# Seven products in place of eight: one Strassen level in the up projection of blocks 1 to 3

## The chip, the cores and the metric

The kernel runs on one core of one Trainium2 chip. The metric is the device time of the whole program in microseconds. Shorter is better. The engines are called here as the profile calls them: PE is the matmul engine (PEld its weight loads), ACT the scalar engine, DVE the vector engine, POOL the GpSimd engine, SP the engine that issues nearly all transfers. Each of them works through its own queue in order.

## The reference, cut to what matters

One decoder layer over 2048 tokens of width 1024, all float32: a gated linear attention mixer beside a cross-attention, an output projection, and then the MLP that the change touches.

```python
def sq_relu_mlp(h, w_up, w_down):
    u = jax.nn.relu(h @ w_up)
    return (u * u) @ w_down
...
    x = x + sq_relu_mlp(rms_norm(x, norm_mlp[i]), w_up[i], w_down[i])
return rms_norm(x, final_norm)
```

Here h is 2048 x 1024, w_up 1024 x 4096 and w_down 4096 x 1024.

## The kernel before

The tokens are taken in four blocks of 512 (block 0 to 3), and each block passes through the mixer, the output projection and the MLP before the next one starts. Every float32 operand is kept as two parts, a high one (`h_hi`, `w_hi`, `u_hi`) that the matmul takes as it is and a low one that holds the remainder (`h_lo`, `w_lo`, `u_lo`). A product of two operands is then three matmuls, high by high, high by low and low by high (`product`, L2171 to L2176); each has a 128 x 128 stationary tile of its own. For weights the parts are made in flight: SP loads a chunk of 1 MB into one of two slots of `raw` (`load`, L739 to L743), ACT copies it into `w_hi` (`split_hi`, L1019, or by halves `split_hi_piece`, L1025), DVE subtracts (`split_lo`, L1517, `split_lo_piece`, L1523). The load of chunk i waits until chunk i - 2 has been split. The two halves of a chunk are its pieces.

The MLP of a block has 16 up chunks of 256 hidden features and 4 groups of 7 down chunks (list `MLP`, L143 to L147). An up chunk multiplies 1024 x 256 weights with 512 tokens, as 2 feature tiles x 8 k-blocks x 3 matmuls of 512 columns, into banks 0 and 1. The down projection already goes by one Strassen (Winograd) level: for each group of 4 up chunks there are 7 products `M1` to `M7` (`PRODUCTS`, L122), each of 24 matmuls of 512 columns. Their operands are three quarters of u (`A11`, `A12`, `A22`) and four sums of quarters (`S1` to `S4`); the sums of the down weights are made once in block 0 by DVE (`mix_sums`, L1504) and kept in DRAM (`w_mix`), and SP issues the loads and stores for them in block 0 (`mix_work`, L767).

Between an up chunk and the down products stands the chain that makes the seven operands of u for one chunk, in the single buffer `u_parts` (8 tiles of 128 x 256): ACT takes relu and square of each bank (`relu_square`, L1384), DVE makes the four sums (`u_sums`, L2028), ACT copies the 3 and the 4 tiles into `u_hi` (`u_high`, L1395), DVE subtracts (`u_low`, L2038, which raises `u_ready`). The next chunk's relu waits for `u_ready` of the chunk before, since it writes `u_parts` again. The operands go into a ring of 5 chunks (`RING`), and the first up chunk of the next group runs ahead of a group's down chunks.

The first up chunk of a block is special (`first_up_chunk`, L2590): it takes its 512 tokens as two halves of 256, since h is only just being transposed, and so has 96 matmuls of 256 columns.

In the MLP, POOL has only small work: reciprocal roots of the norms (`rsqrt`, L912), a diagonal for the next block, and in the last group of blocks 0 to 2 the scaling of the next block's columns (L1010), 8 instructions of 128 x 512.

In the last group of a block PE takes its two first down products by pieces (`last_group_start`, L2664): k-blocks 0, 1 and 2 of both, and then k-block 3 of each, so that the last up chunk has more time to get ready.

## Time and profile before

| | us |
|---|---|
| median of 3 runs | 2530.14 (2529.99 to 2530.43) |
| span of the profiled execution | 2527.2 |
| what lies around the span (2530.14 less 2527.2) | 2.9 |
| PE busy | 2490.0 (99%) |
| DVE busy | 1691.7 (67%) |
| ACT busy | 1247.7 (49%) |
| POOL busy | 345.9 (14%) |
| mean granted clock of PE | 0.999 of full |

The span runs from the first to the last instruction. A busy time is the time in which an engine had an instruction under way. The profiled execution's own device time is not given apart from the span, so the median stands for it: the two differ by 2.9 us, 0.1%. A row of a timeline has the start, the duration, the engine, the line, the operation with what it writes and reads, the shape and how many instructions in a row it merges; in brackets stands idle time before it and what ended that.

### The profile page before, as it was taken

The page shows a single profiled execution, that of the slowest core. Times are in us where ns is not written, and L with a number is a line of the kernel's source. Part 1 is how long each engine was busy: PE and PEld are TensorE (multiplying, and loading weights), DVE is VectorE, ACT ScalarE, POOL GpSimd, SP SyncE. Part 2 cuts the span into 40 slices and gives each one's busy share as a digit, 9 for nine tenths or more (in the row PEclk, how much of TensorE's full clock was granted, in tenths as well). Part 3 has the DMA queues.
Part 4 walks back from the last instruction along what each step waited for, and adds up shares of the span by engine and source line. Part 5 has one row for each costly group of instructions (what it writes and reads, how often), then busy time and mean ns, then how long its engine had stood idle before and what let it go on. Part 6 is the DMA issues. An engine that isn't in the chain of part 4 may idle for free.

```text
span 2527.2 us, 31134 instructions
## 1 busy us (share of the span) xinstructions
PE 2490.0 (99%) x11724; PEld 2087.1 (83%) x11724; DVE 1691.7 (67%) x2473; ACT 1247.7 (49%) x1832; POOL 345.9 (14%) x328
## 2 busy tenths in 40 slices
PE   8999999999999999999999999999999999999998
PEld 7888887888788888888888888888888888888887
DVE  5677467566767786665566778656665687765566
ACT  5544354544554455455455445545455445554344
POOL 0034200000304320000110431000020143000000
PEclk9999999999999999999999999999999999999999
DMA  8522458555732143544442215354444213443443
GB/s 292 183 84 67 157 194 304 182 205 171 261 134 67 51 175 117 190 144 133 166 168 82 67 56 203 100 183 150 150 167 147 70 59 107 160 134 120 164 150 133
DMA packets 201681, 369.48 MB, mean 146 GB/s; under 512 B 8032, under 2 KB 120032, under 8 KB 192576
## 3 DMA queue, kind: packets, MB, share of 16 engines
q1 hardware_dynamic: 200912, 367.25, 43.0%
q8 instruction: 95, 1.56, 0.2%
q14 instruction: 50, 0.41, 0.1%
q10 hardware_dynamic: 624, 0.27, 0.0%
HBM read 336.03 MB, written 31.46 MB: 145 GB/s over the span
## 4 chain that ended last, share of the span: by engine, by line
PE 86%; DVE 5%; DMA 3%; ACT 2%; issue 2%; POOL 1%; DVEq 0%; SPq 0%; ACTq 0%; POOLq 0%
PE banks L2174 25%; PE banks L2175 25%; PE banks L2176 25%; PE banks L2348 3%; POOL queries L946 1%; PE banks L2387 1%; PE banks L2391 1%; PE banks L2327 1%; DVE w_lo L1527 1%; PE banks L2372 1%; PE banks L2304 1%; DMA xres<-in_x 1%; DMA raw<-w_out_mix 1%; DVE xres L1928 0%; DVE query_dec L1679 0%
## 5 line engine op out<-in xcount | busy, mean ns | idle before, releaser
L2174 PE MATMUL banks<-h_hi,w_hi 128*128 128x512 f32 (+1 forms) x1728 | 666.5, 386 | 3.3 <-issue 1.3
L2176 PE MATMUL banks<-h_hi,w_lo 128*128 128x512 f32 (+1 forms) x1728 | 659.0, 381 | 0.0
L2175 PE MATMUL banks<-h_lo,w_hi 128*128 128x512 f32 (+1 forms) x1728 | 659.0, 381 | 0.0
L1527 DVE TENSOR_TENSOR w_lo<-raw,w_hi 128x1024 fp32r<-128x1024 f32 x284 | 357.6, 1294 | 105.2 <-ACT w_hi L1030 97.6
L1520 DVE TENSOR_TENSOR w_lo<-raw,w_hi 128x2048 fp32r<-128x2048 f32 x122 | 292.6, 2398 | 149.2 <-ACT w_hi L1023 145.4
L1030 ACT ACTIVATE w_hi<-raw 128x1024 fp32r<-128x1024 f32 x248 | 253.9, 1053 | 279.3 <-PE banks L2174 93.0
L2174 PEld LDWEIGHTS banks<-h_hi,w_hi 128*128 128x128 f32 x1728 | 324.9, 188 | 66.2 <-issue 4.8
L2176 PEld LDWEIGHTS banks<-h_hi,w_lo 128*128 128x128 f32 x1728 | 324.8, 188 | 63.3
L2175 PEld LDWEIGHTS banks<-h_lo,w_hi 128*128 128x128 f32 x1728 | 325.0, 188 | 60.9
L2174 PE MATMUL banks<-w_hi,u_hi 128*128 128x512 f32 x896 | 350.9, 392 | 2.3 <-DVE w_lo L1527 1.8
L2176 PE MATMUL banks<-w_hi,u_lo 128*128 128x512 f32 x896 | 349.4, 390 | 0.0
L2175 PE MATMUL banks<-w_lo,u_hi 128*128 128x512 f32 x896 | 349.2, 390 | 0.0
L1023 ACT ACTIVATE w_hi<-raw 128x2048 fp32r<-128x2048 f32 x122 | 233.6, 1915 | 145.0 <-PE banks L2174 121.0
L1928 DVE TENSOR_TENSOR xres<-banks,xres 128x512 f32<-128x512 f32 x274 | 182.0, 686 | 75.3 <-PE banks L2176 74.4
L1390 ACT ACTIVATE u_parts<-banks 128x512 f32<-128x512 f32 x128 | 76.2, 595 | 294.7 <-PE banks L2176 163.6
L2174 PEld LDWEIGHTS banks<-w_hi,u_hi 128*128 128x128 f32 x896 | 168.6, 188 | 39.4 <-issue 3.7
L2175 PEld LDWEIGHTS banks<-w_lo,u_hi 128*128 128x128 f32 x896 | 168.6, 188 | 35.4 <-issue 0.7
L2176 PEld LDWEIGHTS banks<-w_hi,u_lo 128*128 128x128 f32 x896 | 168.4, 188 | 35.4
L2033 DVE TENSOR_TENSOR u_parts<-u_parts 128x256 f32<-128x256 f32 x64 | 27.2, 426 | 240.6 <-ACT u_parts L1393 240.6
L946 POOL TENSOR_TENSOR queries<-q,query_dec 128x384 f32<-128x384 f32 x144 | 144.9, 1034 | 175.3 <-ACT query_dec L1172 108.1
L915 POOL TENSOR_TENSOR rstd<-ms,minus_half 128x1 f32<-128x1 f32 x44 | 28.3, 646 | 1027.4 <-DVE ms L1542 1023.2
L2174 PE MATMUL banks<-w_hi,h_hi 128*128 128x512 f32 x392 | 158.8, 405 | 1.6 <-ACT v L1142 1.6
(237 smaller groups left out, 3485.7 us busy)
## 6 DMA issues: line engine op xcount, KB each, us to landing
raw<-in_w_up SPq DMA_DIRECT2D x64, 1024.0 KB, 5.7
raw<-w_mix SPq DMA_DIRECT2D x64, 1024.0 KB, 4.7
raw<-in_gla_w_in SPq DMA_DIRECT2D x56, 1024.0 KB, 5.1
raw<-in_w_down SPq DMA_DIRECT2D x48, 1024.0 KB, 5.1
raw<-w_out_mix SPq DMA_DIRECT2D x24, 512.0 KB, 4.3
raw<-in_w_out SPq DMA_DIRECT2D x21, 512.0 KB, 3.7
xin<-in_w_down SPq DMA_DIRECT2D x10, 1024.0 KB, 5.1
w_mix<-xin SPq DMA_DIRECT2D x10, 1024.0 KB, 5.3
```

Source lines behind the costliest of these rows:

```text
L915: nc.gpsimd.tensor_tensor(rstd[:, which, t:t + 1], ms[:, which, t:t + 1], minus_half[:, 0:1], ALU.pow).then_inc(rstd_ready.sem, 1)
L946: last = nc.gpsimd.tensor_tensor(kind_cols(queries, w, kind), spans(at_chunk(q, c), w, first, count), kind_cols(query_dec, w, kind), ALU.mult)
L1023: nc.scalar.activation(w_hi[:, i % 2, :], raw[:, i % 2, :], ACT.Copy).then_inc(hi_split.sem, PIECES)
L1030: nc.scalar.activation(w_hi[:, i % 2, at], raw[:, i % 2, at], ACT.Copy).then_inc(hi_split.sem, 1)
L1390: nc.scalar.activation(part, banks[:, f, :].rearrange("p (h t) -> p h t", h=2), ACT.Relu)\
L1520: nc.vector.tensor_tensor(w_lo[:, i % 2, :], raw[:, i % 2, :], w_hi[:, i % 2, :].bitcast(F32), ALU.subtract).then_inc(lo_split.sem, PIECES)
L1527: nc.vector.tensor_tensor(w_lo[:, i % 2, at], raw[:, i % 2, at], w_hi[:, i % 2, at].bitcast(F32), ALU.subtract).then_inc(lo_split.sem, 1)
L1928: nc.vector.tensor_tensor(xres[:, t, cols], bank(name), xres[:, t, cols], ALU.add)\
L2174: after_chunk(pe.matmul(to, left[0], right[0], start=start, stop=False, skip_group_check=goes_on))
L2175: pe.matmul(to, left[0], right[1], start=False, stop=False, skip_group_check=goes_on)
L2176: return pe.matmul(to, left[1], right[0], start=False, stop=stop, skip_group_check=goes_on)
L2348: ins = pe.matmul(bank(name)[:, (h % 2) * COLS:(h % 2 + 1) * COLS], left, queries[:, h, :], start=True, stop=True)
```

## The change

Blocks 1 to 3 get another order of steps (`LATE_MLP`). Up chunks 0 and 1 stay as they are. Each up chunk from 2 to 15 becomes two steps, "up a" and "up b", that together make 7 products of 4 k-blocks x 3 matmuls of 256 columns: the tokens are halved (256 and 256), the width of h is halved (4 and 4 k-blocks) and the chunk's 256 features are halved. `M1`, `M6`, `M7` and `M4` are added up in one bank (0 or 7 by turns), `M5` and `M3` share bank 1, and `M2` has bank 6. The output quarters are put together on the way: ACT keeps copies of the bank after `M1`, `M6` and `M5` (`keep_part`), and DVE adds `M2`, `M7` and `M3` to them (`add_part`). The four sums of h are made once a block, two by DVE and two by POOL (both called `h_sums`), and split by ACT and DVE (`s_high`, `s_low`). The squares of three of the u quarters and the four sums of u go from ACT and DVE to POOL (`late_squares`); the fourth quarter is squared by ACT (`corner`). The sums of the up weights are made by POOL in block 0 (`up_mix`, 4 instructions of 128 x 512 a chunk, 14 chunks) and stored to DRAM (`w_up_mix`), and the late steps load them: 1.75 MB a chunk, 0.75 MB of it in runs of 128 columns (512 bytes), where a chunk was 1 MB in runs of 1 KB. The ring of u operands has 4 chunks instead of 5, no up chunk runs ahead of a group's down chunks, and every group of blocks 1 to 3 now starts with the order that only the last group had (`group_start`). The next block's rows of x are loaded one at a time for their squares (`load_x_row`) instead of all at once. Block 0 keeps its steps, with `up_mix` and the stores added; `gain_fin` is loaded later there.

```diff
+
+PLAIN_UPS = 2
+LATE_UPS = UPS - PLAIN_UPS
+LATE_RING = DEPTH
+
+LATE_UP_A = (("M1", A11, 0), ("M2", A12, 1), ("M6", S2, 2), ("M5", S1, 3))
+LATE_UP_B = (("M7", S3, 1), ("M3", S4, 0), ("M4", A22, 2))
+LATE_MLP = []
+for _g in range(GROUPS):
+    for _c in range(DEPTH * _g, DEPTH * (_g + 1)):
+        LATE_MLP += [("up", _c)] if _c < PLAIN_UPS else [("up a", _c), ("up b", _c)]
+    LATE_MLP += [("down", _g, j) for j in range(len(PRODUCTS))]
...
+def late_bank(c, name):
+
+    return {"M2": 6, "M5": 1, "M3": 1}.get(name, 7 if c % 2 else 0)
...
+            def up_mix_store(c):
+
+                sp.wait_ge(up_mix_made, c - PLAIN_UPS + 1)
+                sp.dma_start(w_up_mix[:, c - PLAIN_UPS, 0:2, :], up_mix_t2_t1).then_inc(up_mix_stored, 16)
+                sp.dma_start(w_up_mix[:, c - PLAIN_UPS, 2:4, :], up_mix_t3_t4).then_inc(up_mix_stored, 16)
+
+            def load_late(n, s):
+
+                i, what = OTHERS.mlp + s, LATE_MLP[s]
+                if what[0] not in ("up a", "up b"):
+                    load(n, i, *late_weights(s))
+                    return
+                sp.wait_ge(*hi_split.at(n, last_piece(i - 2)))
+                sp.wait_ge(*lo_split.at(n, last_piece(i - 2)))
+                c, to = what[1], raw[:, i % 2, :]
+                cols = wup[:, :, FCOLS * c:FCOLS * (c + 1)]
+                if what[0] == "up a":
+                    sp.dma_start(to[:, 0:1024].rearrange("p (k c) -> p k c", k=KD), cols[:, :, 0:P])                        .then_inc(up_part_loaded[i % 2].sem, 16)
+                    sp.dma_start(to[:, 1024:2048].rearrange("p (e x) -> p e x", e=2), w_up_mix[:, c - PLAIN_UPS, 0:2, :])                        .then_inc(raw_loaded[i % 2].sem, 16)
+                else:
+                    sp.dma_start(to[:, 0:512].rearrange("p (k c) -> p k c", k=KG), cols[:, KG:KD, P:2 * P])                        .then_inc(up_part_loaded[i % 2].sem, 16)
+                    sp.dma_start(to[:, 512:1536].rearrange("p (e x) -> p e x", e=2), w_up_mix[:, c - PLAIN_UPS, 2:4, :])                        .then_inc(raw_loaded[i % 2].sem, 16)
...
                                 sp.wait_ge(mix_stored[slot], 16 * made)
+                    if s >= 2 and MLP[s - 2][0] == "up" and MLP[s - 2][1] >= PLAIN_UPS:
+                        up_mix_store(MLP[s - 2][1])
...
+                        load_next_columns(n, x_col)
+                        sp.wait_ge(up_mix_stored, 32 * LATE_UPS)
+                        sp.dma_start(gain_fin[:], final_norm.rearrange("(a d) -> a d", a=1).broadcast_to([P, D]))\
+                            .then_inc(gain_fin_loaded, 16)
...
+                def up_mix(s, c):
+
+                    i = FIRST.mlp + s
+                    w = as_kblocks(raw, i % 2, KD)
+                    b11, b12, b21, b22 = (w[:, KG * r:KG * (r + 1), P * f:P * (f + 1)] for r in range(2) for f in range(2))
+                    t2, t1, t3, t4 = (e[:, j, :].rearrange("p (k c) -> p k c", k=KG)
+                                      for e in (up_mix_t2_t1, up_mix_t3_t4) for j in range(2))
+                    pool.wait_ge(*raw_loaded[i % 2].at(n, i // 2))
+                    if c > PLAIN_UPS:
+                        pool.wait_ge(up_mix_stored, 32 * (c - PLAIN_UPS))
+                    pool_link(nc.gpsimd.tensor_tensor(t1, b12, b11, ALU.subtract))
+                    pool_link(nc.gpsimd.tensor_tensor(t2, b22, t1, ALU.subtract))
+                    nc.gpsimd.tensor_tensor(t3, b22, b12, ALU.subtract)
+                    nc.gpsimd.tensor_tensor(t4, b21, t2, ALU.subtract).then_inc(up_mix_made, 1)
+
+                def h_sums():
+
+                    pool.wait_ge(*read(n, ("hT", 1, KD // 2 - 1)))
+                    pool.wait_ge(*read(n, ("hT", 0, KD // 2 - 1)))
+                    a11_hi, a11_lo = (e[:, 0:KG, early_h].bitcast(F32) for e in (h_hi, h_lo))
+                    a21_hi, a21_lo = (e[:, 0:KG, late_h].bitcast(F32) for e in (h_hi, h_lo))
+                    a12_hi, a12_lo = (e[:, KG:KD, early_h].bitcast(F32) for e in (h_hi, h_lo))
+                    nc.gpsimd.tensor_tensor(s3_sum[:], a11_hi, a21_hi, ALU.subtract)
+                    pool_link(nc.gpsimd.tensor_tensor(s3_part[:], a11_lo, a21_lo, ALU.subtract))
+                    nc.gpsimd.tensor_tensor(s3_sum[:], s3_sum[:], s3_part[:], ALU.add).then_inc(s34_sum_ready.sem, 1)
+                    pool.wait_ge(*s12_sum_ready.at(n, 1))
+                    pool_link(nc.gpsimd.tensor_tensor(s4_sum, a12_hi, s2_sum[:], ALU.subtract))
+                    nc.gpsimd.tensor_tensor(s4_sum, s4_sum, a12_lo, ALU.add).then_inc(s34_sum_ready.sem, 1)
+
+                def late_squares(c):
+
+                    a1, b1, b2, a2, s1, s2, s3, s4 = (u_parts[:, e, :] for e in range(8))
+                    k = c - PLAIN_UPS
+                    pool.wait_ge(*relu_ready.at(n, k))
+                    nc.gpsimd.tensor_tensor(u_parts[:, 0:3, :], u_parts[:, 0:3, :], u_parts[:, 0:3, :], ALU.mult)\
+                        .then_inc(body_ready.sem, 1)
+                    pool.wait_ge(*body_ready.at(n, k))
+                    pool.wait_ge(*corner_ready.at(n, k))
+                    pool_link(nc.gpsimd.tensor_tensor(s1, a2, b2, ALU.add))
+                    nc.gpsimd.tensor_tensor(s3, a1, a2, ALU.subtract)
+                    pool_link(nc.gpsimd.tensor_tensor(s2, s1, a1, ALU.subtract))
+                    nc.gpsimd.tensor_tensor(s4, b1, s2, ALU.subtract).then_inc(sums_ready.sem, 1)
+
+                for t in range(TILES):
+                    rsqrt(n, 0, t)
+                if first:
+                    for s, what in enumerate(MLP):
+                        if what == ("up", 2 * DEPTH + 1):
+                            for t in range(TILES):
+                                rsqrt(n, 1, t)
+                            diagonals()
+                        if what[0] == "up" and what[1] >= PLAIN_UPS:
+                            up_mix(s, what[1])
+                else:
+                    h_sums()
+                    for c in range(PLAIN_UPS, UPS):
+                        late_squares(c)
+                        if n < BLOCKS - 1 and c % DEPTH == DEPTH - 1 and c // DEPTH in (1, 2):
+                            for t in range(2 * (c // DEPTH) - 2, 2 * (c // DEPTH)):
+                                rsqrt(n, 1, t)
+                    if n < BLOCKS - 1:
+                        diagonals()
+                if n < BLOCKS - 1:
...
+                def late_up(s, c):
+
+                    ahead = c - 1 if c % DEPTH else None
+                    after = s + 2
+                    if c == PLAIN_UPS:
+                        relu_square(1, 1)
+                    elif ahead is not None:
+                        corner(ahead)
+                    late_split_hi(s + 1, 0)
+                    if c == PLAIN_UPS:
+                        s_high(S4)
+                    keep_part(c, "M1")
+                    late_split_hi(s + 1, 1)
+                    keep_part(c, "M6")
+                    if ahead is not None:
+                        u_high(ahead, False)
+                    late_split_hi(after, 0)
+                    keep_part(c, "M5")
+                    late_split_hi(after, 1)
+                    if ahead is not None:
+                        u_high(ahead, True)
+                    late_relu(c)
+
+                def late_down(s, g, j):
+
+                    c, more = DEPTH * g + DEPTH - 1, s + 1 < len(LATE_MLP)
+                    if j == 0:
+                        corner(c)
+                        late_split_hi(s + 1, 0)
+                        late_split_hi(s + 1, 1)
+                        u_high(c, False)
+                        late_split_hi(s + 2, 0)
+                        u_high(c, True)
+                    elif j == 1:
+                        late_split_hi(s + 1, 1)
...
+                def late_mlp():
+                    split_hi(n, c_mlp + 1)
+                    relu_square(0, 0)
+                    relu_square(0, 1)
+                    late_split_hi(2, 0)
+                    late_split_hi(2, 1)
+                    finish_u(0)
+                    for e in (S1, S3, S2):
+                        s_high(e)
+                    relu_square(1, 0)
+                    for s, what in enumerate(LATE_MLP):
...
+                def h_sums():
+
+                    for half in range(2):
+                        dve.wait_ge(*read(n, ("hT", half, KD // 2 - 1)))
+                    a11_hi, a11_lo = (e[:, 0:KG, early_h].bitcast(F32) for e in (h_hi, h_lo))
+                    a21_hi, a21_lo = (e[:, 0:KG, late_h].bitcast(F32) for e in (h_hi, h_lo))
+                    a22_hi, a22_lo = (e[:, KG:KD, late_h].bitcast(F32) for e in (h_hi, h_lo))
+                    nc.vector.tensor_tensor(s1_sum[:], a21_hi, a22_hi, ALU.add)
+                    link(nc.vector.tensor_tensor(s1_part[:], a21_lo, a22_lo, ALU.add))
+                    nc.vector.tensor_tensor(s1_sum[:], s1_sum[:], s1_part[:], ALU.add).then_inc(s12_sum_ready.sem, 1)
+                    dve.wait_ge(*s12_sum_ready.at(n, 0))
+                    link(nc.vector.tensor_tensor(s2_sum[:], s1_sum[:], a11_hi, ALU.subtract))
+                    nc.vector.tensor_tensor(s2_sum[:], s2_sum[:], a11_lo, ALU.subtract).then_inc(s12_sum_ready.sem, 1)
...
+                def add_part(c, name):
+
+                    e, kept = {"M2": (0, "M1"), "M7": (2, "M5"), "M3": (1, "M6")}[name]
+                    dve.wait_ge(*full(n, ("up", c, name)))
+                    dve.wait_ge(*read(n, ("up", c, kept)))
+                    nc.vector.tensor_tensor(c_parts[:, e, :], bank(("up", c, name))[:, 0:HALF], c_parts[:, e, :], ALU.add)\
+                        .then_inc(bank_read[bank_of(("up", c, name))], 1)
+
+                def late_up(s, c):
+
+                    ahead = c - 1 if c % DEPTH else None
+                    if s and LATE_MLP[s - 1][0] == "down":
+                        add_down(*LATE_MLP[s - 1][1:])
+                    late_split_lo(s + 1, 0)
+                    if c == PLAIN_UPS:
+                        u_sums(1)
+                        s_low(S2)
+                    add_part(c, "M2")
+                    late_split_lo(s + 1, 1)
+                    if c == PLAIN_UPS:
+                        s_low(S4)
+                    if ahead is not None:
+                        u_low(ahead, False)
+                    late_split_lo(s + 2, 0)
+                    add_part(c, "M7")
+                    late_split_lo(s + 2, 1)
+                    if ahead is not None:
+                        u_low(ahead, True)
...
+                def late_mlp():
+                    split_lo(n, c_mlp + 1)
+                    h_sums()
+                    u_sums(0)
+                    late_split_lo(2, 0)
+                    late_split_lo(2, 1)
+                    u_low(0, False)
+                    u_low(0, True)
+                    s_low(S1)
+                    s_low(S3)
+                    for s, what in enumerate(LATE_MLP):
+                        if what[0] == "up a":
+                            late_up(s, what[1])
+                        elif what[0] == "down":
+                            late_down(s, *what[1:])
...
+                def late_products(s, c, *names):
+
+                    part = LATE_UP_A if mlp_steps[s][0] == "up a" else LATE_UP_B
+                    for name, operand, col in part:
+                        if name not in names:
+                            continue
+                        slot, begins = (c_mlp + s) % 2, name in ("M1", "M2", "M5")
+                        if c == PLAIN_UPS and operand >= S1:
+                            pe.wait_ge(*s_lo_ready.at(n, (S1, S3, S2, S4).index(operand)))
+                        pe.wait_ge(*empty(n, ("up", c, name)))
+                        high, low = up_operand[operand]
+                        to = bank(("up", c, name))[:, 0:HALF]
+                        for k in range(KG):
+                            at = slice(col * 512 + k * P, col * 512 + (k + 1) * P)
+                            last = product(to, (w_hi[:, slot, at], w_lo[:, slot, at]), (high[:, k, :], low[:, k, :]),
+                                           begins and k == 0, k == KG - 1, not begins)
+                        last.then_inc(bank_full[bank_of(("up", c, name))], 1)
+
+                def late_up(s, c):
+                    wait_piece(s, 0)
+                    late_products(s, c, "M1", "M2")
+                    pieces_done[0] = 1
+                    wait_piece(s, 1)
+                    late_products(s, c, "M6", "M5")
+                    pieces_done[0] = 1
+                    wait_piece(s + 1, 0)
+                    late_products(s + 1, c, "M7", "M3")
+                    pieces_done[0] = 1
+                    wait_piece(s + 1, 1)
+                    late_products(s + 1, c, "M4")
+                    pieces_done[0] = 1
```

In `late_down` of DVE the first step of a group is: split both halves of the next chunk, `u_low` of three quarters, split the first half of the chunk after it, `u_low` of the sums. ACT has the same order (above).

## Rows read from the trace of the kernel before

**Rows 1.** The page's busy times: engine, busy us, share, instructions.

```profile
PE 2490.0 (99%) x11724; PEld 2087.1 (83%) x11724; DVE 1691.7 (67%) x2473; ACT 1247.7 (49%) x1832; POOL 345.9 (14%) x328
```

**Rows 2.** Timeline of PE, block 1, first up chunk (256 columns) and second (512).

```profile
966.01 0.28 PE L2174 MATMUL banks<-h_hi,w_hi 128*128 128x256 f32 x1
...
972.72 0.28 PE L2176 MATMUL banks<-h_hi,w_lo 128*128 128x256 f32 x1
...
973.61 0.40 PE L2176 MATMUL banks<-h_hi,w_lo 128*128 128x512 f32 x1
...
984.52 0.39 PE L2176 MATMUL banks<-h_hi,w_lo 128*128 128x512 f32 x1
```

**Rows 3.** Timelines of ACT and of DVE over one up chunk of block 1.

```profile
985.43 1.90 ACT L1023 ACTIVATE w_hi<-raw 128x2048 fp32r<-128x2048 f32 x1
987.24 0.83 ACT L1403 ACTIVATE u_hi<-u_parts 128x768 fp32r<-128x768 f32 x1
987.97 1.05 ACT L1399 ACTIVATE u_hi<-u_parts 128x1024 fp32r<-128x1024 f32 x1
991.83 0.60 ACT L1390 ACTIVATE u_parts<-banks 128x512 f32<-128x512 f32 x1 [2.81 <-DVE u_lo L2047]
...
985.63 0.42 DVE L2033 TENSOR_TENSOR u_parts<-u_parts 128x256 f32<-128x256 f32 x1 [4.68 <-ACT u_parts L1393]
...
987.43 2.29 DVE L1520 TENSOR_TENSOR w_lo<-raw,w_hi 128x2048 fp32r<-128x2048 f32 x1
989.64 2.09 DVE L2047 TENSOR_TENSOR u_lo<-u_parts,u_hi 128x768 fp32r<-128x768 f32 x2
```

**Rows 4.** Timeline of POOL, then of DVE, where POOL scales the next columns (block 1).

```profile
1256.76 16.35 POOL L1010 TENSOR_TENSOR next_x<-next_x,xin 128x512 f32<-128x512 f32 x8 [125.97 <-ACT xin L1462]
...
1256.15 3.19 DVE L2047 TENSOR_TENSOR u_lo<-u_parts,u_hi 128x768 fp32r<-128x768 f32 x2
1259.27 2.31 DVE L1527 TENSOR_TENSOR w_lo<-raw,w_hi 128x1024 fp32r<-128x1024 f32 x1
1261.50 1.27 DVE L1928 TENSOR_TENSOR xres<-banks,xres 128x512 f32<-128x512 f32 x2
...
1265.03 3.44 DVE L1527 TENSOR_TENSOR w_lo<-raw,w_hi 128x1024 fp32r<-128x1024 f32 x2
```

**Rows 5.** Timeline of POOL in the mixer of block 1, DVE idle or in PSUM work.

```profile
789.56 0.75 POOL L940 TENSOR_TENSOR queries<-q,near_dec 128x256 f32<-128x256 f32 x1 [4.22 <-PE banks L2348]
790.27 1.30 POOL L956 TENSOR_TENSOR q<-q,query_dec 128x512 f32<-128x512 f32 x1
```

**Rows 6.** Groups by line and shape: busy us, mean ns of one, idle before.

```profile
L1648 DVE TENSOR_TENSOR mem_lo<-banks,mem_hi 128x256 fp32r<-128x256 f32 x32 | 12.4, 421 | 1.9 <-ACT mem_hi L1161 1.9
...
L1161 ACT ACTIVATE mem_hi<-banks 128x256 fp32r<-128x256 f32 x32 | 12.0, 387 | 3.0 <-PE banks L2327 3.0
```

**Rows 7.** Timeline of DVE at the start of the MLP of block 1.

```profile
965.42 3.23 DVE L1943 SCALAR_TENSOR_TENSOR h_lo<-banks,gain_mlp,h_hi 128x256 fp32r<-128x256 f32 x8 [1.62 <-ACT h_hi L1352]
969.48 2.29 DVE L1520 TENSOR_TENSOR w_lo<-raw,w_hi 128x2048 fp32r<-128x2048 f32 x1 [0.83 <-ACT w_hi L1023]
```

**Rows 8.** Timeline of PE in block 0, after a gap.

```profile
407.83 0.47 PE L2174 MATMUL banks<-w_hi,u_hi 128*128 128x512 f32 x1 [1.84 <-DVE w_lo L1527]
...
408.79 0.63 PE L2174 MATMUL banks<-w_hi,u_hi 128*128 128x512 f32 x1
...
411.78 0.40 PE L2175 MATMUL banks<-w_lo,u_hi 128*128 128x512 f32 x1
```

**Rows 9.** Stretches of block 0: busy us of PE, PEld, DVE, ACT, POOL, clock, DMA share, GB/s.

```profile
360.00:375.00 15.00, 15.00 (x67) 12.40 (x67) 10.59 (x15) 7.87 (x10) 0.00 (x0) 1.00 0.90 314
405.00:420.00 15.00, 12.70 (x48) 9.71 (x47) 9.38 (x12) 3.85 (x4) 0.00 (x0) 0.89 0.93 349
```

**Rows 10.** Timeline of SP in block 0: issue of the second down chunk's load.

```profile
388.82 0.41 SPq L743 DMA_DIRECT2D raw<-w_mix  x1
```

**Rows 11.** The page's DMA issues: count, KB each, median us from issue to landing.

```profile
raw<-in_w_up SPq DMA_DIRECT2D x64, 1024.0 KB, 5.7
```

479 lines of the change are left out of this document (346 added, 133 removed).

## The prediction

> **What bounds the kernel now.** I read the page's busy times first: PE is busy 99% of the span, DVE 67%, ACT 49%, POOL 14% [rows 1]. So time falls only if PE's work falls, and it grows wherever another engine's queue falls behind PE. Then I read PE's timeline for what one matmul takes in a row of them: 57 starts of 256 columns from 966.01 to 972.72, (972.72 - 966.01) / 56 = 0.1198 us; 49 starts of 512 columns from 973.61 to 984.52, 10.91 / 48 = 0.2273 us [rows 2]. Half the columns cost 53% of the time. Last I read the timelines of ACT, DVE and POOL, since they get new work.
>
> **What PE gains.** An up chunk is 48 x 0.2273 = 10.91 us. Seven products are 7 x 12 = 84 matmuls of 256 columns, 84 x 0.1198 = 10.06 us. That is 0.85 us less a chunk, 42 chunks: -36 us if nothing else holds PE (7.8% of an up chunk, not the eighth that the count of products suggests). The Trainium skill (TensorE: Matmul & The Clock Gate, Back-to-back issue gap) gives N / 2.4 GHz + 2.5 ns for an isolated gap, 109 and 216 ns; by that the gain would be 42 x (48 x 0.2158 - 84 x 0.1092) = 50 us. The rows have 120 and 227, and the sum goes by them.
>
> **What a POOL instruction costs DVE.** While POOL scales columns, 8 instructions take 16.35 us, 2.04 each, against 1.30 for one of the same size in quiet [rows 4, 5]. Read beside DVE's rows they take turns. DVE's subtraction of 1024 from two SBUF tiles, about 1.2 us alone (half of 2.29 [rows 3]), takes 2.31; a pair of `u_low` takes 3.19 in place of 2.09 [rows 3, 4]; a pair of subtractions takes 3.44. The addition that reads PSUM keeps its 1.27 for two. 8 x 1.28 of POOL plus the some 6 us of DVE's two-tile work in that stretch is 16.3: whole instructions of the one wait for whole instructions of the other. The Trainium skill (SBUF — State Buffer, SBUF: two separate sides) calls it an exclusive lock, held for the full instruction, between GpSimd and a DVE instruction with two SBUF inputs. By that rule and by the row the sum below is the same; if they shared without loss, it would be the first rival. DVE's new adds (`add_part`) read PSUM and are free of it.
>
> **Durations for the walks.** Spacing in a queue: ACT 1024 columns 0.95 (half of 985.43 to 987.24 for 2048, plus the start), 768 0.73, 512 0.54; DVE 1024 1.13, 768 0.9, 512 0.6, 256 0.34 to 0.42 [rows 3]; 256 columns from PSUM 0.39 on ACT, 0.42 on DVE [rows 6]; POOL 256 0.75, 512 1.3 [rows 5], by their line 768 1.8 and 1024 2.35 (not in the trace; bounds 1.3 x 1.5 = 1.95 and 1.3 x 2 = 2.6 above, 1.3 below). 0.1 for a handover.
>
> **A steady late chunk.** Port work is 4.6 us of POOL (1.8 and 4 x 0.7) and 5.9 us of DVE (3 halves, a quarter, two `u_low`): 10.5 us, more than PE's 10.06. And the chain from one `late_relu` to the next goes once through all queues. ACT: `corner` 0.8, four splits, three `keep_part`, two `u_high`, 7.6 us if nothing is late; then `u_low` and `M3`'s add on DVE and the relu, 1.8: 9.5 in all. With turns taken at the port, `u_high` of the sums finds POOL's four sums late. I walked the four chunks of a group (us from PE's start of each):
> - c0, nothing ahead: relu ends at 10.03. PE 10.06.
> - c1: POOL squares to 1.9, sums 2.0, 3.9, 5.2, 6.8 to 7.5, each behind a DVE split or `u_low`; DVE gets `M7` added at 8.95, so `M4`, which adds to the same bank, starts at 9.0 instead of 8.62. Relu ends 12.4. PE 10.45.
> - c2: relu ended at 1.95. ACT's order puts `corner` and a split ahead of keeping `M1`, so that is kept at 4.0, and `M6`, which goes into `M1`'s bank, waits from 2.88 to 4.05. Sums end 10.5, relu 14.05. PE 11.55.
> - c3: relu ended at 2.5; PE 12.1 by the same steps.
> - Down: `corner`, two splits, squares, sums, `u_high`, `u_low`, with POOL and DVE by turns, end 12.8 to 13.9 after c3. PE starts the second product at 5.55 instead of 4.08 and wants the sums at 11.0: it ends its two products at about 14.8 instead of 10.9.
> Against 10.91 each: -0.85, -0.46, +0.64, +1.2, +3.9 = +4.4 us a group. Nine groups (1 to 3 of three blocks): +40. The lower bound, all of POOL in DVE's gaps, is -2 us a group, -18.
>
> **The start of blocks 1 to 3.** `h_low` ends at 968.65 and DVE splits chunk 1 at 969.48 [rows 7]. New between there and PE's end of chunk 1 at 984: 5 instructions of 1024 on DVE (5.7 us) and 5 on POOL (11.7), then `u_sums`, two splits, `u_low`, which stand in the queue behind them. DVE is never without port work from 969.5 to 990, so all five of POOL's come in between: POOL 968.8-971.1, DVE 971.1-973.3, POOL 975.6, DVE 976.7, POOL 979.0, DVE to 983.7, POOL 986.1, DVE 986.9, POOL 989.3, `u_sums` ends 990.2. ACT waits in order for these sums; `u_low` ends 994.5, and only then may relu empty bank 0, which the first late product wants. PE starts it at 995.3 instead of 984. `M6` then waits for the low part of `S2`, behind a split and `u_sums` of chunk 1, till 1002. Chunk 2 ends at 1009.2; before, 994.8. +14.4, and +4.5 for chunk 3 and its down chunks: 19 x 3 = +57. Without turns at the port the same walk gives +3.6, and then about zero: +11.
>
> **Block 0.** POOL's `up_mix` is 4 x 1.3 = 5.2 us of port a chunk beside DVE's 5.8 (8.2 with `mix_sums`) in 10.91. The sums have one buffer (`tail`, `gain_fin`), so the next `up_mix` waits for the store, and SP, in order, waits for `up_mix` ahead of the second next load. The DMA queues are at 0.90 of their time in the first up chunks, and PE already waited 1.84 us there [rows 8, 9]. Three stores of 1 MB more, and SP held by `up_mix` of chunk 4 till about 404 where the load of the second down chunk went out at 388.82 [rows 10]: with some 7.5 us to land PE waits about 12, of which it later had 5 to lose anyway: +7. The other groups I take at +2 to +3: +14 together, bounds 0 (all in slack) and 35.
>
> **The clock.** After the gap of 1.84 us the matmuls stand 0.43 us apart from 408.79 to 411.35: half speed, 1.2 GHz, and full again at 411.78; the stretch has 0.89 [rows 8, 9]. That cost 8 x 0.2 = 1.6 us. The late groups' down start has a gap of 1.9 to 3 us: 12 x 1.6 = +19 (bounds 0 and, if chunk gaps of 1.2 to 1.7 do it too, +50).
>
> **At nothing.** Loads: 1.75 MB a late chunk; a 1 MB load in runs of 1 KB lands in 5.7 us [rows 11], runs of 512 bytes may take up to twice, and the tightest load ("up b") has about 8 us. If this is wrong, 1 to 3 us a chunk come on top. The scaling of the next columns starts some 7 us later, with splits that wait in DVE's queue; the x rows' loads and squares lie beside down chunks.
>
> **Sum.** 40 + 57 + 14 + 19 = +130; the gain of 36 is inside the walks. 2530.14 + 130 = **2660 us**. The walks are made on the profiled execution, 2.9 us of which lie outside the span, and those don't change.
>
> **The rivals.**
> - The port costs nothing because POOL's work falls in DVE's gaps. For: POOL's 4.6 us are short pieces. Against: [rows 4], and DVE's unbroken queue at block start. 11 - 18 + 8 (block 0) = +1: 2531.
> - Only the block starts and block 0 are late, the groups hold: 57 + 14 = +71, less 9 x 2 = 18: 2585 (up to 2600).
> - Faster: PE is the bound everywhere. This decides where the chain between two relus stays under 10.06 us (uncontended it is 9.5, so half a microsecond decides) and the sums of h end before 984. -36 and some 6 for the low pace after single gaps: 2500.
> - Heavier: clock falls in most late chunks, or 512-byte loads late: 42 x 1.5 more: 2720.
>
> **Chances.** Forecast 0.56; start only 0.16; port free 0.13; heavier 0.08; faster 0.07. Its own range is 2610 to 2700; 8 in 10 need the start-only case too and some of the space below it: 2550 to 2710. What this kernel's measurement can tell from no change is about 0.2%, 5 us. Faster: 0.07 and a quarter of the port-free case, 0.10; same, half of that case, 0.07; slower 0.83.
>
> **What would show it.** Right: matmuls of 256 columns 0.12 apart; POOL busy some 600 us more; DVE's subtractions of 1024 averaging well over 1.3 us; PE idle 10 us before the first late chunk in each of three blocks; idle of 2 to 3 us at each group's second down product with the granted clock below 1 there; late chunks lasting 10.1, 10.5, 11.5, 12. Wrong: a mean late chunk under 10.5 us, or DVE's rows unchanged beside POOL's, and then the port step has failed; PE waiting for `raw` loads, and then the step at nothing has.

## The result, and the profile after

| | us |
|---|---|
| before, median of 4 runs | 2530.13 (2529.99 to 2530.43) |
| after, median of 4 runs | 2637.85 (2634.57 to 2644.38) |
| after to before | 1.0426, 95% interval 1.0411 to 1.0441 |
| span of the profiled execution after | 2634.0 (before 2527.2: +106.8) |

The change costs 4.3%. The page of the changed kernel has these busy times, to be laid beside [rows 1]:

```profile
PE 2490.7 (95%) x13236; PEld 2146.1 (81%) x13236; DVE 1886.0 (72%) x2584; ACT 1328.5 (50%) x2054; POOL 742.5 (28%) x609
```

PE is busy for the same time as before, 2490 us, though its 42 late chunks are less work: most of what they save came back, as shown below, as half speed behind long waits (some 16 us) and as slow first matmuls behind waits (1.45 us a group, by run 12). What has grown is the time in which it stands. The waits of PE by what ended them (us in total, times, the longest) name the places:

```profile
PE banks L2638 <- ACT u_parts L1601: 34.4, 7, 9.9
PE banks L2638 <- ACT c_parts L1672: 20.3, 21, 1.0
PE banks L3102 <- POOL late_diag L1145: 16.5, 2, 8.2
PE banks L2638 <- issue: 13.4, 5, 7.1
PE banks L2638 <- ACT w_hi L1656: 12.7, 10, 1.5
```

I cut the 106.8 us by place. The transposes of h start the MLP of each block. Their first rows in PE's timeline, after and then before:

```profile
986.26 1.97 PE L3042 MATMUL banks<-ident,hn 128*128 128x128 f32 x16 [0.88 <-DVE hn L1895]
...
1632.95 0.33 PE L3042 MATMUL banks<-ident,hn 128*128 128x128 f32 x1 [0.89 <-DVE hn L1895]
...
2279.38 0.33 PE L3042 MATMUL banks<-ident,hn 128*128 128x128 f32 x1 [0.88 <-DVE hn L1895]
```

```profile
963.85 0.33 PE L2577 MATMUL banks<-ident,hn 128*128 128x128 f32 x1 [0.88 <-DVE hn L1546]
...
1579.27 0.33 PE L2577 MATMUL banks<-ident,hn 128*128 128x128 f32 x1 [0.88 <-DVE hn L1546]
...
2195.67 0.33 PE L2577 MATMUL banks<-ident,hn 128*128 128x128 f32 x1 [0.88 <-DVE hn L1546]
```

Up to block 1's MLP the change has lost 986.26 - 963.85 = 22.4 us (block 0); from there to block 2's, 646.7 against 615.4, +31.3; to block 3's +30.0; from there to the end +23.1.

**A block's start.** PE's timeline at chunk 2 of block 1, the first late chunk:

```profile
1017.03 0.55 PE L2638 MATMUL banks<-h_hi,w_hi 128*128 128x256 f32 x1 [9.93 <-ACT u_parts L1601]
1017.38 0.41 PE L2639 MATMUL banks<-h_lo,w_hi 128*128 128x256 f32 x1
...
1022.08 0.41 PE L2640 MATMUL banks<-h_hi,w_lo 128*128 128x256 f32 x1
1023.96 0.36 PE L2638 MATMUL banks<-s_hi,w_hi 128*128 128x256 f32 x1 [1.47 <-DVE s_lo L2495]
```

A wait of 9.93 us, then 24 matmuls 0.21 apart where [rows 2] have 0.12: half speed, (0.21 - 0.12) x 24 = 2.2 us more, then a wait for the low part of `S2`. What PE waits for is seen in POOL's and in DVE's timeline just before:

```profile
991.13 2.40 POOL L1179 TENSOR_TENSOR s_sum<-h_hi 128x1024 f32<-128x1024 f32 x1 [5.72 <-DVE h_lo L2292]
993.49 4.46 POOL L1180 TENSOR_TENSOR s_part<-h_lo 128x1024 f32<-128x1024 f32 x1
...
1006.23 2.47 POOL L1183 TENSOR_TENSOR tail<-h_hi,s_sum 128x1024 f32<-128x1024 f32 x1 [4.95 <-DVE s_sum L2484]
```

```profile
991.89 3.80 DVE L1869 TENSOR_TENSOR w_lo<-raw,w_hi 128x2048 fp32r<-128x2048 f32 x1 [0.84 <-ACT w_hi L1234]
995.61 3.42 DVE L2479 TENSOR_TENSOR s_sum<-h_hi 128x1024 f32<-128x1024 f32 x1
998.95 3.42 DVE L2480 TENSOR_TENSOR s_part<-h_lo 128x1024 f32<-128x1024 f32 x1
1002.41 1.22 DVE L2481 TENSOR_TENSOR s_sum<-s_sum,s_part 128x1024 f32<-128x1024 f32 x1
...
1006.52 2.46 DVE L2383 TENSOR_TENSOR u_parts<-u_parts 128x256 f32<-128x256 f32 x1
```

While POOL has an instruction, the same subtraction and addition of DVE last 3.80 and 3.42 where they last 2.29 [rows 7] and 1.22 alone, and an addition of 256 columns 2.46 in place of 0.42: the two wait for each other's whole instructions. From the start of chunk 1 (995.95) to that of chunk 4 (1082.97) pass 87.0 us; before it is 3 up chunks and 7 down chunks, 3 x 10.9 + 38.1 = 70.8 us. That is +16.2 in block 1. By the same reading it is +17.4 in block 2, where the wait for `S2` is 2.15 us and half speed comes a second time behind it, and +16.2 in block 3: +49.8 for the three.

**A steady group.** The first matmul of a group's first up chunk and that of the next group, in block 1, after and then before:

```profile
1167.00 0.28 PE L2638 MATMUL banks<-h_hi,w_hi 128*128 128x256 f32 x1
...
1250.79 0.28 PE L2638 MATMUL banks<-h_hi,w_hi 128*128 128x256 f32 x1
```

```profile
1054.78 0.39 PE L2174 MATMUL banks<-h_hi,w_hi 128*128 128x512 f32 x1
...
1136.38 0.39 PE L2174 MATMUL banks<-h_hi,w_hi 128*128 128x512 f32 x1
```

83.8 against 81.6 us: +2.2 a group, nine of them +20. Its four up chunks last 10.1, 10.2, 11.6 and 11.6 us, together 43.5 as before, so the first two gain what the last two lose. The +2.2 stand at the down start, where PE waits 1.24 and 0.41 us. The stretch of this group (busy us of PE, PEld, DVE, ACT, POOL, clock, DMA share, GB/s):

```profile
1167.00:1250.79 83.79, 79.95 (x506) 71.95 (x504) 59.88 (x66) 46.71 (x66) 26.18 (x22) 1.00 0.55 189
```

The third and fourth chunk of each group have the wait that 21 rows like this one hold (`M6` for the copy after `M1`):

```profile
1107.27 0.36 PE L2638 MATMUL banks<-s_hi,w_hi 128*128 128x256 f32 x1 [1.02 <-ACT c_parts L1672]
```

**The last group of blocks 1 and 2.** POOL's timeline from the squares of chunk 15, and PE's below it:

```profile
1296.34 1.47 POOL L1191 TENSOR_TENSOR u_parts<-u_parts 128x768 f32<-128x768 f32 x1 [5.11 <-ACT u_parts L1680]
...
1303.32 3.43 POOL L1145 TENSOR_TENSOR late_diag<-ident,rstd 128x128 f32<-128x128 f32 x4
```

```profile
1306.80 2.08 PE L3102 MATMUL banks<-late_diag,ones 128*128 128x512 f32 x2 [8.24 <-POOL late_diag L1145]
1307.89 1.42 PE L2638 MATMUL banks<-w_hi,u_hi 128*128 128x512 f32 x1
```

The diagonal of the next block's norms stands last in POOL's queue; PE wants it in the middle of the group's first down products and has all of them queued behind it. No step of my prediction has this. What is left of blocks 1 and 2 when starts and groups are taken off, 31.3 - 16.2 - 6.6 and 30.0 - 17.4 - 6.6, is 8.5 and 6.0: 14.5 us for both. It is a remainder, and run 1 below measures it.

**Block 0.** PE waits 7.06 us at 402 to 409 (before 1.84 [rows 8]) and 5.37 at 449 to 454 (before 1.27):

```profile
409.45 0.77 PE L2638 MATMUL banks<-w_hi,u_hi 128*128 128x512 f32 x1 [7.06 <-issue]
...
454.40 0.77 PE L2638 MATMUL banks<-h_hi,w_hi 128*128 128x512 f32 x1 [5.37 <-issue]
```

DVE's and POOL's timelines ahead of the second:

```profile
444.06 1.78 DVE L1860 TENSOR_TENSOR xin<-xin 128x512 f32<-128x512 f32 x1
...
449.27 1.63 DVE L1863 TENSOR_TENSOR xin<-xin 128x512 f32<-128x512 f32 x1
```

```profile
443.15 2.15 POOL L1167 TENSOR_TENSOR tail<-raw 128x512 f32<-128x512 f32 x1 [47.41 <-DMA raw<-in_w_up]
...
448.65 1.71 POOL L1170 TENSOR_TENSOR gain_fin<-raw,tail 128x512 f32<-128x512 f32 x1
```

`mix_sums` of the down weights, 4 x 0.69 us in the kernel before, takes 4 x 1.7 beside `up_mix`, strictly by turns, and the split that PE waits for stands behind it in DVE's queue.

So 22.4 + 49.8 + 9 x 2.2 + 14.5 and 0.3 left in block 3 = 106.8.

**Half speed lies inside these parts.** The granted clock is 0.50 in eight stretches of the MLPs. Their sum (us, then the busy us of each engine):

```profile
sum 71.60, PE 38.78 PEld 32.79 DVE 48.76 ACT 39.09 POOL 14.30; mean PE 4.85 PEld 4.10 DVE 6.10 ACT 4.89 POOL 1.79
```

PE was busy for 38.8 us of them, before it was for 3.4 (408.4 to 411.8). Matmuls stand 0.21 us apart there in place of 0.12, or 0.43 in place of 0.23, so some 0.45 of that time is lost: 0.45 x (38.8 - 3.4) = 16 us.

### The profile page after: what moved, and what is told of

Same layout as the page of the kernel before. It is cut to its first block, busy times and chain, and to the rows that moved or that the text cites. A ratio compares the mean times of both kernels' runs of the same rounds, so it can differ in the third digit from the quotient of the medians.

```text
span 2634.0 us, 35778 instructions
## 1 busy us (share of the span) xinstructions
PE 2490.7 (95%) x13236; PEld 2146.1 (81%) x13236; DVE 1886.0 (72%) x2584; ACT 1328.5 (50%) x2054; POOL 742.5 (28%) x609
## 4 chain that ended last, share of the span: by engine, by line
PE 68%; DVE 11%; ACT 7%; issue 7%; POOL 5%; DMA 2%; ACTq 0%; DVEq 0%; SPq 0%; POOLq 0%
PE banks L2638 20%; PE banks L2640 19%; PE banks L2639 19%; DVE u_lo L2396 3%; PE banks L2813 3%; ACT w_hi L1656 2%; POOL queries L1092 1%; DVE w_lo L1876 1%; PE banks L2852 1%; PE banks L2856 1%; PE banks L2792 1%; PE banks L2837 1%; DVE c_parts L2502 1%; PE banks L2769 1%; POOL u_parts L1197 1%
## 5 line engine op out<-in xcount | busy, mean ns | idle before, releaser
L1876 DVE TENSOR_TENSOR w_lo<-raw,w_hi 128x1024 fp32r<-128x1024 f32 x410 | 543.9, 1351 | 212.2 <-ACT w_hi L1656 164.1
L2638 PE MATMUL banks<-h_hi,w_hi 128*128 128x512 f32 (+1 forms) x1728 | 602.1, 348 | 45.4 <-ACT u_parts L1601 34.4
L2639 PE MATMUL banks<-h_lo,w_hi 128*128 128x512 f32 (+1 forms) x1728 | 591.6, 342 | 0.0
L2640 PE MATMUL banks<-h_hi,w_lo 128*128 128x512 f32 (+1 forms) x1728 | 591.3, 342 | 0.0
L1656 ACT ACTIVATE w_hi<-raw 128x1024 fp32r<-128x1024 f32 x294 | 303.7, 1052 | 180.9 <-PE banks L2638 79.3
L1869 DVE TENSOR_TENSOR w_lo<-raw,w_hi 128x2048 fp32r<-128x2048 f32 x80 | 204.8, 2560 | 118.2 <-ACT w_hi L1234 117.9
L1191 POOL TENSOR_TENSOR u_parts<-u_parts 128x768 f32<-128x768 f32 x42 | 61.6, 1467 | 484.0 <-ACT u_parts L1680 484.0
L1234 ACT ACTIVATE w_hi<-raw 128x2048 fp32r<-128x2048 f32 x80 | 153.5, 1918 | 82.0 <-PE banks L2638 61.1
L2638 PE MATMUL banks<-s_hi,w_hi 128*128 128x256 f32 x504 | 145.1, 288 | 25.4 <-ACT c_parts L1672 20.3
L2396 DVE TENSOR_TENSOR u_lo<-u_parts,u_hi 128x768 fp32r<-128x768 f32 (+1 forms) x128 | 152.4, 1203 | 21.6 <-ACT u_hi L1617 21.1
```

The source lines that it names most:

```text
L1191: nc.gpsimd.tensor_tensor(u_parts[:, 0:3, :], u_parts[:, 0:3, :], u_parts[:, 0:3, :], ALU.mult)\
L1234: nc.scalar.activation(w_hi[:, i % 2, :], raw[:, i % 2, :], ACT.Copy).then_inc(hi_split.sem, PIECES)
L1656: nc.scalar.activation(w_hi[:, i % 2, at], raw[:, i % 2, at], ACT.Copy).then_inc(hi_split.sem, 1)
L1869: nc.vector.tensor_tensor(w_lo[:, i % 2, :], raw[:, i % 2, :], w_hi[:, i % 2, :].bitcast(F32), ALU.subtract).then_inc(lo_split.sem, PIECES)
L1876: nc.vector.tensor_tensor(w_lo[:, i % 2, at], raw[:, i % 2, at], w_hi[:, i % 2, at].bitcast(F32), ALU.subtract).then_inc(lo_split.sem, 1)
L2396: nc.vector.tensor_tensor(u_lo[:, c % ring(n), at, :], source, u_hi[:, c % ring(n), at, :].bitcast(F32), ALU.subtract).then_inc(u_ready.se ...
```

## The experiments

Twelve kernels, all built on the changed one. Ratios are to the kernel before; a difference in us is between medians unless it says span.

**1. The diagonal made early.**

```diff
                             for t in range(2 * (c // DEPTH) - 2, 2 * (c // DEPTH)):
                                 rsqrt(n, 1, t)
-                    if n < BLOCKS - 1:
-                        diagonals()
+                            if c // DEPTH == 2:
+                                diagonals()
```

> The changed kernel with one move: POOL makes the diagonal of reciprocal norms for the next block right after the last of its reciprocal roots (after the squares of chunk 11) and not behind the squares and sums of chunk 15. My prediction had no term for this wait. Theory A (it is a real wait of PE, 8.24 us in the profile in blocks 1 and 2, and the half-speed matmuls behind it): 2 x (8.2 + 1 to 2) = 18 to 20 us less, 2638 to about 2619, and no wait on late_diag in the profile. Theory B (the wait only shows a place where the last down chunk's operands or the load would have been late anyway): the same gap comes back under another name, 0 to 4 us less.

2623.91 us, 1.0365 (1.0347 to 1.0382): 13.9 less, close to the 14.5 that were left over. The wait on `late_diag` is gone in both blocks; in the same stretch stand waits of 0.38, 0.38 and 0.48, so a little of the 8.2 comes back. Theory A in kind, three quarters of its size.

**2. The copy after M1 ahead of the split.**

```diff
                         corner(ahead)
+                    if c != PLAIN_UPS:
+                        keep_part(c, "M1")
                     late_split_hi(s + 1, 0)
                     if c == PLAIN_UPS:
                         s_high(S4)
-                    keep_part(c, "M1")
+                        keep_part(c, "M1")
```

> The changed kernel with ACT's order in a late chunk altered: the copy of the bank after M1 comes right behind the corner and ahead of the split of the next half chunk (chunk 2 excepted). My step said that this order makes PE wait 1.2 us before M6 in c2 and c3 of a group (the profile has 1.02 and 1.01). Theory A (the order is the cause, and nothing else is late): these 21 gaps shrink from 1.0 to about 0.2 and the program gets 21 x 0.8 = 17 us shorter. Theory B (the chain from relu to relu is as long as PE's wait makes it, 11.62 us a chunk, and only 0.45 of it can be won before POOL's sums hold u_high): gaps of c2 and c3 are gone, the gap at the group's down start grows from 1.25 to about 2, 10 to 13 us shorter. Theory C (neither): no change.

2639.43 us, 1.0426 (1.041 to 1.0441): no change. The 21 waits are still there, under another name. Waits of PE in this kernel:

```profile
PE banks L2640 <- DVE c_parts L2504: 21.8, 21, 1.1
```

The third and fourth chunk of a group still last 11.6 us. This is Theory C, and it is the most useful miss: the wait was ended by ACT's copy, but it was not caused by ACT's order alone. It belongs to a ring (relu, squares, ACT's and DVE's rows of work, the next relu), and PE waits at whichever link it meets first.

**3. The four sums of u on DVE.**

```diff
-                    pool_link(nc.gpsimd.tensor_tensor(s1, a2, b2, ALU.add))
...
                     add_part(c, "M2")
+                    if ahead is not None and c > PLAIN_UPS:
+                        u_sums(ahead)
```

> The changed kernel with the four sums of u of each late chunk made by DVE (behind the addition of M2; at a group's down start behind the first split) in place of POOL, which keeps only the squares. Theory A (whole instructions of POOL and of DVE's work on two SBUF tiles take turns at one port): DVE's subtraction of 1024 columns falls from 1.6 back to 1.2 us beside the late chunks, the four sums take 0.42 each in place of 0.74 to 1.6, the sums at a down start are ready some 1.5 us earlier and the second product starts 0.5 to 1 us earlier; c2 and c3 keep their gap of 1.0, which is ACT's order; 5 to 12 us less in all. Theory B (no shared port, DVE is simply full): DVE has 1.7 us more a chunk, the additions of M7 and M3 come later and late chunks get 0.5 to 1.5 us longer, 20 to 60 us more.

2614.54 us, 1.0326 (1.0311 to 1.0342): 23.3 less with more work on DVE. DVE's timeline in a late chunk, of the changed kernel and of this one:

```profile
1106.96 1.66 DVE L1876 TENSOR_TENSOR w_lo<-raw,w_hi 128x1024 fp32r<-128x1024 f32 x1 [2.79 <-ACT w_hi L1656]
```

```profile
1106.09 1.23 DVE L1870 TENSOR_TENSOR w_lo<-raw,w_hi 128x1024 fp32r<-128x1024 f32 x1 [2.79 <-ACT w_hi L1650]
...
1107.57 0.42 DVE L2380 TENSOR_TENSOR u_parts<-u_parts 128x256 f32<-128x256 f32 x1
```

The subtraction is back at 1.2. A group takes 82.7 in place of 83.8 us, 9 x 1.1 = 10, as Theory A said. But its third and fourth chunk still last 11.4 us, so POOL's sums were not what made them long. The rest of the gain is for the most part that POOL, rid of the sums, gets to the diagonal earlier: that wait falls from 8.24 to 2.09 in both blocks.

**4. All sums of h on DVE** (POOL's five instructions put behind DVE's five in `h_sums`).

> The changed kernel with all ten instructions for the sums of h at the start of blocks 1 to 3 on DVE, none on POOL. Theory A (my step: POOL's five, 2.4 us each, are in the way of DVE at a shared port, so that the two queues together last as long as their sum): DVE's first split goes from 3.8 back to 2.3, its sums from 3.4 to 1.2, and the ten end at about 1006.5 on the scale where u_sums now ends at 1011.9; the wait before the first late chunk falls from 9.9 to about 6, 3 x 4 = 12 us less, a little more if the clock comes back. Theory B (the engines do not disturb each other and u_sums is late because of what stands before it in DVE's queue): five more instructions put it 6 us later, the wait grows to 16 us, 18 us more in all.

2628.35 us, 1.0384 (1.0369 to 1.04): 9.5 less. In this execution block 1 begins 2.6 us later than in the one shown above (988.8 against 986.3). The ten instructions on DVE end at 1008.7, 1006.1 on the other scale, where POOL's five ended at 1011.2. DVE's and PE's timelines:

```profile
996.66 1.22 DVE L2478 TENSOR_TENSOR s_sum<-h_hi 128x1024 f32<-128x1024 f32 x1
...
1007.50 1.23 DVE L2490 TENSOR_TENSOR tail<-tail,h_lo 128x1024 f32<-128x1024 f32 x1
```

```profile
1015.42 0.55 PE L2644 MATMUL banks<-h_hi,w_hi 128*128 128x256 f32 x1 [6.26 <-ACT u_parts L1600]
```

The wait falls from 9.93 to 6.26, by moving work onto the engine that is late. Theory A. By the Trainium skill (SBUF — State Buffer, SBUF: two separate sides) GpSimd and a DVE instruction with two SBUF inputs exclude each other for a full instruction; the runs agree, 3.42 beside POOL and 1.22 without.

**5 and 6. Block 0: POOL's work without its weight, and the sums without their stores.** The first cuts the sums to 2 of 128 columns from the second chunk on, the second leaves the stores out and loads other weights of the same size in the late chunks; what either computes is not the reference's result.

```diff
+                    wide = P if c == PLAIN_UPS else 2
+                    t1, t2, t3, t4, b11, b12, b21, b22 = (e[:, :, 0:wide] for e in (t1, t2, t3, t4, b11, b12, b21, b22))
```

```diff
-                        up_mix_store(MLP[s - 2][1])
+                        sp.wait_ge(up_mix_made, MLP[s - 2][1] - PLAIN_UPS + 1)
...
```

> The changed kernel with POOL's weight sums in block 0 cut to 2 of 128 columns a k-block from the second chunk on (the stores of 1 MB stay whole, so the late chunks read sums that are not the reference's): work left out. It takes POOL away from DVE's side in block 0 and keeps the bytes and SP's order. Block 0 with the mixer costs 22.4 us more than before. Theory A (my step: the stores and the loads behind them cost the 7 us gap at 402 to 409, turns at the port are small): 3 to 6 us less. Theory B (the port is the larger half, as DVE's mix_sums of 4 x 1.7 in place of 4 x 0.7 at 444 to 451 suggest): 8 to 14 us less, the gap of 5.37 at 454 falls to about 1.3, and the one of 7.06 at 409 loses only 1 to 2. The late loads and all of blocks 1 to 3 stay as they are.

> The changed kernel without the stores of the weight sums in block 0; POOL makes them all, SP still waits for each, and the late chunks load other weights of the same size from another array (so the result is not the reference's): work left out. It takes 14 MB of writes and 28 issues away and keeps the port as it is. Theory A (the transfers cost the gap at 402 to 409): that gap falls from 7.06 to 2 or 3, since POOL no longer waits for the store either; 6 to 12 us less. Theory B (the port): 2 to 4 us less, and the gap of 5.37 at 454 stays. Together with the run that keeps the stores and cuts POOL's work the two should give about the 22 us.

5: 2627.78 us, 1.0385 (1.0369 to 1.0402), 10.1 less; `mix_sums` is back at 4 x 0.69 us, the wait at 454 is 1.28 again, that at 409 stays at 6.93. 6: 2636.39 us, 1.0422 (1.0405 to 1.0438), 1.5 less, which the spread of the changed kernel (2634.57 to 2644.38) does not tell from nothing; the wait of 5.37 stays, that of 7.06 is 3.92, but POOL, which no longer waits for its stores, now makes sums earlier and new waits of 1.53 and 4.42 appear (at 375 and 560). So the port makes about half of block 0's loss. The other half I put down to the transfers and to SP's queue, but no run shows it: 10.1 and 1.5 don't add up to 22, as my expectation had it.

**7. SP's order: the load ahead of the stores.**

```diff
...
+                    if stores:
+                        sp.wait_ge(up_mix_made, MLP[s - 2][1] - PLAIN_UPS + 1)
+                    load(n, c_mlp + s, *mlp_source(s))
+                    if stores:
                         up_mix_store(MLP[s - 2][1])
-                    load(n, c_mlp + s, *mlp_source(s))
```

> The changed kernel with SP's order in block 0 altered alone: the load of a chunk is issued ahead of the two stores of weight sums and not behind them (SP still waits for POOL's sums first, since the load goes over the chunk that they read). Theory A (the loads are late because their data wait behind 1 MB of stores in the queues): the load lands 1 to 2.5 us earlier, the wait at 409 goes from 7 to about 5, the one at 454 is unchanged, 2 to 4 us less. Theory B (SP's wait for POOL is what is late, or the queues' total): within 1 us of no change.

2666.22 us, 1.0539 (1.052 to 1.0558): 28.4 more. Both theories fail. Waits of 10.83 (at 414), 6.32 (515) and 10.31 (611) stand in PE's timeline. The sums have one buffer: POOL's next sums wait for the store, and SP's next load waits for POOL's sums. A store that goes out after the load lands later, so POOL starts later, and SP with it. I read this from the queues; no run takes it apart.

**8. All orders together** (1, 2 and 3, and three more).

```diff
 # ACT, late chunk: u_high(ahead, True) ahead of late_split_hi(after, 1)
 # ACT, down start: late_split_hi(s + 1, 0) ahead of corner(c)
 # DVE, late chunk:
                     add_part(c, "M7")
-                    late_split_lo(s + 2, 1)
                     if ahead is not None:
                         u_low(ahead, True)
                     add_part(c, "M3")
+                    late_split_lo(s + 2, 1)
```

> The changed kernel with the diagonal made early, the sums of u on DVE, the copy after M1 ahead of the split, and three more orders in blocks 1 to 3: ACT rounds the sums of u before the second split of the next chunk, DVE adds M3 and subtracts the sums before its second split, and at a group's down start ACT splits before the corner. The copy after M1 alone gained nothing (the wait went over to DVE's addition of M7), the sums on DVE alone 23 us. Theory A (one ring runs through relu, squares, ACT's and DVE's queues and back to relu, 11.6 us in c1 to c3; each order shortens it, so only together do they bring it below PE's 10.06): the gaps of c2 and c3 fall to 0 to 0.3, the down start keeps 0.3, a group takes 79.5 to 80 us in place of 83.8, which is below the 81.8 of before; 9 x 3.9 and 3 x 2 and 14 for the diagonal, about 55 us less: 2580 to 2588. Theory B (ACT or DVE is simply full in a late chunk, no order helps): a group stays at 82.5 or more and the time at about 2600.

2591.89 us, 1.024 (1.0224 to 1.0256). A group takes 80.9 us, 0.7 less than before the change; its first chunk lasts 10.07 and the other three 10.9, not 10.06. DVE works without a gap from 1105.45 to the addition of `M7` at 1111.11, and its first row waits for ACT. Between the two theories, nearer to A.

**9. Late form from chunk 4 on.** `PLAIN_UPS` is `DEPTH`; the sums of h stand on DVE behind chunks 0 to 2 and at down product 2 of group 0.

> The version with all orders of the run before, and the late form only from chunk 4 on (12 chunks a block in place of 14): the ten instructions for the sums of h all stand on DVE, three or two behind each of chunks 0 to 2 and at the third down product of group 0, their rounding and remainders at down products 3 to 6; DVE adds M7 ahead of the first split of the next chunk. Block 0 makes 12 chunks of weight sums, so none beside chunks 2 and 3. Theory A (the start of a block cost 9.9 us because ten instructions had to fit between two up chunks, and it disappears when they have four chunks and seven down products; block 0's crunch at 402 to 409 is half made by the sums of chunks 2 and 3): no gap over 1 us at the starts, 3 x (9.9 + 1.5 + 2.3 of half-speed matmuls) = 41 us less, 3 x 2 x 0.85 = 5 more for the chunks that go back, block 0 some 8 to 12 less; against 2588 of the run before about 2543, range 2535 to 2555: still not faster than before. Theory B (the gain of the late chunks now carries it): under 2530. It needs a group of 79.5 us and block 0 at under 10 us of loss.

2545.86 us, 1.0054 (1.004 to 1.0068), 46 less than run 8, Theory A within 3 us. No wait at a block's start is left. Block 0 still loses 984.96 - 963.85 = 21.1, so that the two chunks of sums that went away there were worth 1 to 2 us only (22.4 in the changed kernel, 23.5 in run 8), not 8 to 12: there the expectation was wrong.

**10 and 11. The split ahead of the corner, with the late form from chunk 8 and from chunk 4.**

```diff
+                    late_split_hi(s + 1, 0)
                     if ahead is not None:
                         corner(ahead)
                     keep_part(c, "M1")
-                    late_split_hi(s + 1, 0)
```

> Late form only from chunk 8 on (the last two groups of blocks 1 to 3, 8 chunks a block), with every order of the version before and one more: ACT splits the next half chunk right behind the relu, ahead of the corner and the copy of M1, because DVE's row of work from that split to the addition of M3 (7.6 us without a gap) waits for it. Block 0 makes weight sums only for chunks 8 to 15. Theory A (three separate costs, all with a cure: block 0's sums fall beside its own mixing of the down weights in chunks 0 to 4 only, so with chunks 8 to 15 it loses about 3 us; a group gets to 79.5 us against 81.8, six groups -14; 18 chunks gone back cost nothing against before): 2530 + 3 - 14 = about 2519, 2512 to 2526, faster than the kernel before. Theory B (the orders do not shorten the ring further and a late group stays at 81.0): 2530 + 3 - 5 = 2528, no difference that shows.

> The version with the late form from chunk 4 on and only ACT's split moved ahead of the corner and the copy of M1. Theory A (the ring from relu to relu was 10.87 us: relu, corner, copy and split 3.1 on ACT, then 7.6 of DVE; with the split in front it is about 9.8, under PE's 10.06): the gaps of 1.2 to 1.5 in the last chunk of each group fall under 0.4, a group takes 79.2 to 79.8 in place of 81.0, 9 x 1.5 = 13 us less, 2546 to about 2532. Theory B (PE's M6 then waits for the copy of M1 instead, as the wait moved when that copy was moved alone): 0 to 5 less.

11: 2545.3 us, 1.0059 (1.0046 to 1.0072), the same as run 9. Waits of 0.41 for the copy of `M1` took the place of the one of 1.45: Theory B. 10: 2555.19 us, 1.0096 (1.008 to 1.0111), slower than both expectations. Block 0 did what was expected (+5.1), and block 3 is 2.4 us shorter than before. But in blocks 1 and 2 I had packed the four loads of rows of x into one group and a half, and SP waits in its queue with the next loads of weights behind it. For the first row it waits until DVE has subtracted the low part of `S4`, since `S4` and the rows of x share the buffer `tail`; for the third and fourth it waits for ACT's square of the row before. SP's timeline (its load before these two went out at 1104.96), DVE's row that it waited for, SP's waits from 1100 to 1300, and PE's timeline:

```profile
1114.38 0.33 SPq L866 DMA_DIRECT2D tail<-in_x  x1
1114.81 0.39 SPq L835 DMA_DIRECT2D raw<-in_w_down  x1
```

```profile
1113.14 1.22 DVE L2507 TENSOR_TENSOR h_lo<-tail,h_hi 128x1024 fp32r<-128x1024 f32 x1
```

```profile
SPq L866 <- ACT junk L1688: 21.4, 2, 10.8
SPq L866 <- DVE h_lo L2507: 9.1, 1, 9.1
```

```profile
1123.63 0.47 PE L2661 MATMUL banks<-w_hi,u_hi 128*128 128x512 f32 x1 [3.71 <-ACT w_hi L1649]
...
1199.55 0.77 PE L2661 MATMUL banks<-w_hi,u_hi 128*128 128x512 f32 x1 [4.51 <-ACT w_hi L1649]
```

So of the two waits of PE, 3.71 follows from `S4` and 4.51 from a square; what I expected of run 12 names a square for both.

**12. The last version.** From run 10; the rows of x spread over three groups, `S4` summed behind chunk 4, so that the first row of x has the buffer before it, and its low part subtracted one down product earlier, the copy of `M1` ahead of the corner, `M7` added behind the split.

```diff
-X_LOADS = {("down", 1, 4): 0, ("down", 2, 0): 1, ("down", 2, 2): 2, ("down", 2, 4): 3}
+X_LOADS = {("down", 0, 2): 0, ("down", 1, 4): 1, ("down", 2, 0): 2, ("down", 2, 4): 3}
...
                     late_split_hi(s + 1, 0)
+                    keep_part(c, "M1")
                     if ahead is not None:
                         corner(ahead)
-                    keep_part(c, "M1")
```

> The late form from chunk 8 on, with three edits to the run that had it so and lost: the rows of x for the next block are loaded at down products 2 of group 0, 4 of group 1 and 0 and 4 of group 2 (there SP stood in its queue for a square that ACT had not reached, and PE waited 3.7 and 4.5 us); ACT copies M1 ahead of the corner; DVE again adds M7 behind the first split of the next chunk, which now has its operand in time. Theory A (each wait named is the whole of its gap, and the ring through relu, M1's copy, M6, M7, M3 and back, 10.6 us, comes under PE's 10.06): no gap over 1 us in blocks 1 to 3, late chunks 10.1 each, a late group 78.6 to 79.2 us against 81.8; block 0 stays at 5 over before: 2530 + 5 - 6 x 2.9 = about 2518, 2512 to 2524. Theory B (the ring moves on to another link, as it did with each single edit): late group 80.5 to 81, 2527 to 2531, no difference that shows.

2519.36 us, 0.9946 (0.9933 to 0.996): faster than the kernel before, by 11.9 us, and 118 us faster than the change as made. A late group, in PE's timeline of block 1, and the stretch of it (busy us of PE, PEld, DVE, ACT, POOL, clock, DMA share, GB/s):

```profile
1133.55 0.28 PE L2665 MATMUL banks<-h_hi,w_hi 128*128 128x256 f32 x1
...
1212.03 0.28 PE L2665 MATMUL banks<-h_hi,w_hi 128*128 128x256 f32 x1
```

```profile
1133.50:1212.00 78.50, 78.50 (x505) 71.82 (x505) 61.79 (x82) 47.01 (x66) 10.69 (x12) 1.00 0.59 202
```

78.5 us with no wait at all: 3.1 less than the 81.6 before, 0.78 a chunk (the groups of blocks 2 and 3 take 78.8). This is the gain that I put at 0.85, seen free of waits. PE is busy 1.45 us less than in the same group of the changed kernel, whose 79.95 stand beside four waits. No run has these orders with more late chunks. My estimate from runs 9 and 12 is that it would not pay: the sums of 12 chunks cost block 0 some 13 us more than those of 8, and three more groups at 78.5 to 78.8 give 8 to 9 back.

## Why the prediction was right, and where its steps were off

The forecast was 2660, its range 2550 to 2710; measured are 2637.85. By its own sum it had +130 and the runs have +107. The nearness is partly luck: two terms were too large, one was too small, one stood in the wrong place, and one was missing.

- **What PE gains** (0.85 a chunk): right, 0.78 in run 12. The matmuls of 256 columns are 0.12 apart, as [rows 2] said.
- **What a POOL instruction costs DVE**: right. Runs 3, 4 and 5 each take POOL's work away from DVE's and each gets faster, the first two although DVE has more to do. Two of the signs that I named came out weak: POOL is busy 397 us more, not some 600, and DVE's subtractions of 1024 average 1.35 us, where they had 1.29 before.
- **The start of blocks** (+57 for three, and a share of the clock term): right in place and kind, 9.9 us of wait where the walk had 11.3; +50 for three with the half-speed matmuls in it.
- **A steady late chunk** (+40 for nine groups, and 14 of the clock term): right that `M6` waits for the copy of `M1` and that the down start is late; the size was wrong, +20 in all. c1 lasts 10.2 us where the walk had 10.45, and c2 and c3 last the same 11.6, where the walk let the delay grow from 11.55 to 12.1. POOL's squares take 1.47 us, not the 1.8 that I took, below the bound of 1.95 from 512 columns, and the down start costs 2.2 (waits of 1.25 and 0.4), not 3.9. I also took the chain between two relus for 9.5 us without turns at the port. Run 3, rid of POOL's sums, has 11.4 and run 8, with other orders as well, 10.9; only with the orders of run 12 do the last two chunks of a group last 10.1.
- **Block 0** (+14, bounds 0 and 35): 22.4, and with weight sums for 14, 12 and 8 chunks 22.4, 21.1 and 5 to 8 (runs 9, 10 and 12). The wait that I placed at the second down chunk (12, of which 5 would be lost later anyway) is there with 7.06. The term of +2 to +3 for each other group was too low: DVE's `mix_sums` beside `up_mix` at 444 to 451 is a clash that my sum did not walk through. How the rest divides between bytes and SP's queue stays open.
- **The clock** (+19 by 12 down starts): wrong in place, and near in size by luck. The granted clock is 1.00 from 1103 to 1127, with two gaps of 1.0 in it, and the down starts with 1.25 to 1.5 run at full speed behind them. Half speed follows the long waits instead: 0.53 from 1017 to 1023, 0.70 from 1308 to 1316, and so behind each wait of 5.4 us and more in the MLPs; of the shorter ones, one of 2.15 in block 2 has it too, one of 2.02 at 427 has not. It cost about 2.2 us at the start of blocks 1 and 3 and some 16 in all, which the terms above and below hold.
- **The missing term**: `diagonals()` went in the diff from an early place in POOL's queue to behind chunk 15's squares, and PE waits for it with everything queued behind: +14.5, of which run 1 took 13.9 back. My walks followed the operands of the products and never asked what else stood in POOL's queue.
- **At nothing** (loads with runs of 512 bytes): right: the loads with such runs are those of `in_w_up`, 512 KB in 4.0 us and 256 KB in 2.8 (medians of the DMA view; the 512 KB of `w_up_mix` beside them land in 4.7), and no wait of PE in blocks 1 to 3 of the changed kernel is put down to a load.

The rival "faster" named its condition well (the chain between two relus under PE's 10.06 and the sums of h in time); run 12 meets both, by other orders and 8 late chunks a block in place of 14, and is faster.

## What to carry to other kernels

A saving of 7% on the busiest engine's up chunks was worth nothing here until the ring of the helper engines around it was shorter than its new pace. A wait that moves to another name when you cure it, as in runs 2 and 11, says that it belongs to a ring; the group came down from 83.8 to 78.5 us only by edits at several of its links. Before giving work to an idle POOL, look at what DVE does at that moment: where both worked from two SBUF operands, their times added, and DVE alone was faster (runs 3 and 4: 1.22 us on DVE for what took POOL 2.40). For each instruction that a diff moves in a queue, list what other engine waits for it, however small it is (the diagonal: 3.4 us of work in each of two blocks, some 14 us lost).

## What was not expected of the hardware

POOL's product of 768 columns with itself takes 1.47 us, hardly more than one of 512 columns from two tiles (1.30 [rows 5]), so its time is not in proportion to columns across forms. A short wait costs PE some 0.2 us more than itself: over the wait of 1.02 at 1107.27 the starts stand 1.30 apart and the next 0.19, in place of 0.12 each.
